# RWKV preparation of half 0 run beside the GLU blocks of the odd projection

## The reference

```
def odd_layer(x, ...):
    p = rms_norm(x, norm_g) @ w_in
    u, z_c, feat, z_d = split_cols(p, ODD_SIZES)
    y_c = jax.nn.gelu(s5_ssm(u, ...) + d_skip * u)
    g_a, g_b = jnp.split(y_c @ w_glu, 2, axis=-1)
    o_c = g_a * jax.nn.sigmoid(g_b) * jax.nn.silu(z_c)
    prev = jnp.pad(feat, ((0, 0), (1, 0), (0, 0)))[:, :-1]
    feat = feat + (prev - feat) * mu
    r, k, v, wd, ad = split_cols(feat, (512, 512, 512, 64, 64))
    o_d = rwkv7_time_mix(r, k, v, wd, ad, ...) * jax.nn.silu(z_d)
    return x + jnp.concatenate([o_c, o_d], axis=-1) @ w_out

def rwkv7_time_mix(r, k, v, wd, ad, ...):       # its start, what "preparation" computes
    w = -jax.nn.softplus(-(w0 + jnp.tanh(wd) @ w2)) - 0.5
    decay = jnp.exp(-jnp.exp(w))
    a = jax.nn.sigmoid(a0 + ad @ a2)
    kk = l2norm((k * k_k).reshape(bsz, T, H, Dh))
    k = k * (1.0 + (a - 1.0) * k_a)
    ...                                          # scan over tokens, group norm
    bonus = jnp.sum(rh * kh * r_k, axis=-1, keepdims=True) * vh
```

## Time and profile before

| | |
|---|---|
| median of three runs | 1521.49 us |
| the profiled execution | 1514.38 us, of which span 1512.6 us |
| PE busy | 1300.0 us (86%) |
| DVE busy | 891.8 us (59%) |
| ACT busy | 480.4 us (32%) |
| POOL busy | 308.6 us (20%) |
| projection of the odd layer, last matmul | about 1049.2 us |
| stage of preparation half 0 | 1053.2 to 1110.6 us |
| stage of `invert` half 0 and preparation half 1 | 1110.6 to 1206.8 us |

### The profile page before, as it was taken

How to read it: one execution, slowest core, us unless ns; L and a number is a source line. 1 busy time by engine, 2 the same in 40 slices (tenths; PEclk the granted TensorE clock), 3 DMA queues, 4 the chain that set the end, 5 groups by cost and what they waited for, 6 DMA issues and landing times. The chain is left out here.

```text
span 1512.6 us, 20654 instructions
## 1 busy us (share of the span) xinstructions
PE 1300.0 (86%) x8498; PEld 1079.1 (71%) x8498; DVE 891.8 (59%) x1191; ACT 480.4 (32%) x822; POOL 308.6 (20%) x156
## 2 busy tenths in 40 slices
PE   4999999899779869959997999998343798999698
PEld 4677888778569848848886888886122587889587
DVE  5277754920266573159975664943778787265841
ACT  5234254221346651132431122321652312122310
POOL 2232212211023372031211111220300400000420
PEclk9999999989899969989999999999655699689899
DMA  5212112320300032232331435221000000010523
GB/s 185 43 43 66 42 36 71 97 71 15 140 22 2 2 139 79 103 81 86 98 99 47 114 79 167 63 75 66 0 1 1 1 1 2 13 45 2 195 84 111
DMA packets 117558, 97.79 MB, mean 65 GB/s; under 512 B 37016, under 2 KB 102680, under 8 KB 117336
## 3 DMA queue, kind: packets, MB, share of 16 engines
q1 hardware_dynamic: 103832, 77.45, 17.1%
q10 hardware_dynamic: 13632, 19.01, 3.8%
HBM read 70.23 MB, written 24.51 MB: 63 GB/s over the span
## 5 line engine op out<-in xcount | busy, mean ns | idle before, releaser
L167 PE MATMUL banks<-xt_lo,w_hi 128*128 128x512 f32 x816 | 323.3, 396 | 6.3 <-POOL w_lo L497 6.3
L168 PE MATMUL banks<-xt_hi,w_lo 128*128 128x512 f32 x816 | 319.7, 392 | 0.0
L169 PE MATMUL banks<-xt_hi,w_hi 128*128 128x512 f32 x816 | 319.4, 391 | 0.0
L497 POOL TENSOR_TENSOR w_lo<-features,w_hi 128x1024 fp32r<-128x1024 f32 x55 | 149.4, 2717 | 525.6 <-ACT w_hi L506 525.6
L167 PEld LDWEIGHTS banks<-xt_lo,w_hi 128*128 128x128 f32 x816 | 154.4, 189 | 41.9 <-POOL w_lo L497 6.8
L169 PEld LDWEIGHTS banks<-xt_hi,w_hi 128*128 128x128 f32 x816 | 154.4, 189 | 32.9
L168 PEld LDWEIGHTS banks<-xt_hi,w_lo 128*128 128x128 f32 x816 | 154.6, 189 | 31.2
L550 ACT ACTIVATE temporaries<-banks 128x1024 f32<-128x1024 f32 x47 | 56.0, 1192 | 328.3 <-PE banks L169 320.3
L506 ACT ACTIVATE w_hi<-features 128x1024 fp32r<-128x1024 f32 x55 | 57.8, 1054 | 27.9 <-PE banks L169 26.7
L167 PE MATMUL banks<-xt_lo,oout_mh 128*128 128x512 f32 x128 | 50.8, 397 | 12.6 <-DVE xt_lo L1581 12.6
L295 PE MATMUL banks<-temporaries,features 128*128 128x128 f32 x256 | 35.7, 299 | 26.3 <-DVE temporaries L272 26.3
(11 more groups left out here) (451 smaller groups left out, 2618.8 us busy)
## 6 DMA issues: line engine op xcount, KB each, us to landing
features<-in_even_w_in SPq DMA_DIRECT2D x26, 512.0 KB, 3.8
features<-in_odd_w_in SPq DMA_DIRECT2D x25, 512.0 KB, 4.3
features<-in_x SPq DMA_DIRECT2D x8, 512.0 KB, 7.4
even_gates<-temporaries ACTq DMA_DIRECT2D x8, 512.0 KB, 2.6
features<-even_gates SPq DMA_DIRECT2D x8, 512.0 KB, 8.9
features<-in_even_w_out SPq DMA_DIRECT2D x8, 512.0 KB, 3.4
temporaries<-in_x SPq DMA_DIRECT2D x8, 512.0 KB, 4.7
h_between_layers<-features SPq DMA_DIRECT2D x8, 512.0 KB, 2.9
```

The costliest lines, as they stand in the source:

```text
L167: nc.tensor.matmul(out, w[0], x[1], start=start, stop=False)
L168: nc.tensor.matmul(out, w[1], x[0], start=False, stop=False)
L169: return nc.tensor.matmul(out, w[0], x[0], start=False, stop=stop)
L497: nc.gpsimd.tensor_tensor(wl[n % 2], wr[n % NW], wh[n % 2].bitcast(F32), ALU.subtract).then_inc(low, 1)
```

## The change

The v3 block is put ahead of the four GLU blocks (it is block 24 now, the GLU blocks are 25 to 28), so that all RWKV features and the normed input are done with when the GLU begins. A GLU block is now two units: all matmuls of the gate part into banks 2 and 3, then all of the value part into banks 0 and 1. Banks 4 to 7 are free, and the preparation of half 0 is put beside the GLU blocks in them, with the due times of `BESIDE_GLU`; its stage of its own is gone. Its tiles move into the area in which the normed input lay. For this the v3 block is written into a temporary, and the preparation of half 1 copies it to its place with one ACT instruction more. Of the semaphores, 33 are now cleared on POOL during the projection, and those of the projection and of preparation half 0 (90) at the start of the `invert` stage, where 32 were cleared before.

```diff
+                    def glu_unit(part):
+                        for h in range(2):
+                            for k in range(WB):
+                                hs, kw = slice(h * 512, (h + 1) * 512), WB * part + k
+                                last = three_passes(nc, co.ps[:, 2 * part + h, :], (wh[n % 2][:, kw, :], wl[n % 2][:, kw, :]),
+                                                    (glu["x"][0][k][:, hs], glu["x"][1][k][:, hs]), k == 0, k == WB - 1)
+                        return last
+
                     if glu_no[n] == 0:
                         pe.wait_ge(glu["low"], WB)
...
+                    else:
+                        pe.wait_ge(tanhed, post_no[n - 1] + 1)
+                    glu_unit(1).then_inc(gates_made, 1)
+                    aside.upto(n - 0.5)
+                    if glu_no[n] == 0:
+                        pe.wait_ge(evacuated, evac_no[n - 1] + 1)
+                    else:
+                        pe.wait_ge(finished, post_no[n - 1] + 1)
+                    last = glu_unit(0)
...
+                    if glu_no[n]:
+                        spill(n - 1)
+                    act.wait_ge(gates_made, glu_no[n] + 1)
+                    act.wait_ge(finished, post_no[n])
+                    nc.scalar.activation(t_.rearrange("p (h t) -> p h t", h=2), banks(2), ACT.Tanh, scale=0.25).then_inc(tanhed, 1)
+                    aside.upto(n - 0.25)
...
+BESIDE_GLU = dict(
+    tensor=dict(gates=(24.5, 25), sums=25.5, bonus=(25.5, 26), spread=26.5, pairs=lambda c: 29),
+    scalar=dict(start=24, gates=(24.75, 25.5), root=25.75, decay=(25.75, 26.5), high=26, slices=lambda c: 29),
+    gpsimd=dict(shift=(27, 27.5), rate=(28, 28), zero=29),
+    vector=dict(start=24, scan=(24.75, 25.5), centre=(25, 25.5), keys=(25, 25.5), root=25.75, low=26, decay=(26, 27), normal=(26.75, 26.75),
+                second=(27, 27.5), late=(27, 27.5), kept=lambda c: 29))
...
-    banks = lambda i: co.ps[:, 2 + 2 * (i % 3):4 + 2 * (i % 3), :]
+    banks = lambda i: co.ps[:, 2 + 2 * (i % 3):4 + 2 * (i % 3), :] if half else co.ps[:, 4 + 2 * (i % 2):6 + 2 * (i % 2), :]
...
+            if not half and i >= 2:
+                pe.wait_ge(tanhed, i - 1)
...
-            if c >= 3:
-                pe.wait_ge(kept, c - 2)
+            if c >= (3 if half else 2):
+                pe.wait_ge(kept, c - 2 if half else c - 1)
...
+        if half:
+            nc.scalar.activation(x.v[:, 1, :], x.v3_made, ACT.Copy).then_inc(v_placed, 1)
...
-    blocks += [(P * b, "glu", oc[b]) for b in range(WB)] + [(at("v", 3), "shift", v[3])]
+    blocks += [(P * b, "glu", oc[b]) for b in range(WB)]
...
+    cleared = clearing(co, at=2.5, done=(first_load, last_load))
...
+    project(co, "op", a["odd_w_in"][0], blocks, mu=a["rwkv_mu"][0], beside=together(s5, r7_prepare(co, first, BESIDE_GLU), cleared),
...
-    side_by_side(co, clearing(co), r7_prepare(co, first, 0))
-    side_by_side(co, clearing(co), invert(co, "ri0", first.n_st, R7_INVERT[0]), r7_prepare(co, second, 33))
+    side_by_side(co, clearing(co), invert(co, "ri0", first.n_st, R7_INVERT[0]), r7_prepare(co, second, beside_preparation(33)))
```

More of the change, by code:

```diff
@@ L97, in sem, with done_sems @@
         return handle
+    def done_sems(self, first, last):
+        old, self.taken = self.taken[:first] + self.taken[last:], self.taken[first:last]
+        return old
     def old_sems(self):
@@ L556, in _ @@
                     spill(n)
-                if n in post_no:
+                if n in post_no and n not in glu_no:
                     if kind == "conv":
@@ L2146, in clearing, with beside_preparation, r7_prepare @@
     return dict(gpsimd=gpsimd, old=old)
-def r7_prepare(co, x, d):
+def beside_preparation(d):
+    return dict(
+        tensor=dict(gates=(0, 0), sums=8, bonus=(d + 6.5, d + 12.5), spread=d + 14.5, pairs=lambda c: d + 30 + c),
+        scalar=dict(start=0, gates=(1, 8), root=9, decay=(d + 8, d + 14), high=d + 13, slices=lambda c: d + 31 + c),
+        gpsimd=dict(shift=(d + 6, d + 12), rate=(d + 17, d + 19), zero=d + 26),
+        vector=dict(start=0, scan=(d, d + 6), centre=(d + 2, d + 8), keys=(d + 4, d + 10), root=d + 12, low=d + 13.5, decay=(d + 15, d + 18.5), normal=(d + 16.5, d + 17.5),
+                    second=(d + 22, d + 25), late=(d + 23.5, d + 26.5), kept=lambda c: d + 30.5 + c))
+BESIDE_GLU = dict(
[4 more added lines that the diff above has]
+                second=(27, 27.5), late=(27, 27.5), kept=lambda c: 29))
+def r7_prepare(co, x, paces):
     nc = co.nc
@@ L2205, in tensor @@
         for j in range(2):
-            if j:
-                pe.wait_ge(bout, 1)
+            if not half or j:
+                pe.wait_ge(bout, j if half else j + 1)
             for h in range(2):
                 hs = slice(512 * h, 512 * h + 512)
-                nc.tensor.matmul(banks(1 + j)[:, h, :], pairs[:, j, :], low[:, hs], start=True, stop=False)
-                last = nc.tensor.matmul(banks(1 + j)[:, h, :], pairs[:, j, :], high[:, hs], start=False, stop=True)
+                nc.tensor.matmul(banks(spread_at[j])[:, h, :], pairs[:, j, :], low[:, hs], start=True, stop=False)
+                last = nc.tensor.matmul(banks(spread_at[j])[:, h, :], pairs[:, j, :], high[:, hs], start=False, stop=True)
             last.then_inc(spread, 1)
         for c in range(NT):
-            yield d + 30 + c
+            yield at["pairs"](c)
             if c == 0:
```

199 lines of the change are left out of this document (114 added, 85 removed).

## The result

The changed kernel takes 1479.88 us (median of four, 1474.99 to 1484.29) against 1522.13 on the same chip: a ratio of 0.973, 95% interval 0.971 to 0.9745. The prediction was 1494.2 us and a gain of 27.3; the gain is 42.2 here, and in two more measurements of the same kernel 35.5 (ratio 0.979, 0.974 to 0.984) and 35.2 (0.976, 0.974 to 0.978). The profiled execution took 1474.99 us, with a span of 1473.2.

A forecast was written before the change was run, and what follows sets the result against it. TensorE bounds the GLU blocks; the preparation's own stage is a chain of waits. Added 14.4 + tail 15.4 - 61.4 replaced = -31.6; clears +4.3 make -27.3, so 1521.49 becomes 1494.2 us, range 1489 to 1505.

The forecast's parts named there:

- the rival of the clock: GLU stretch: waits before the units bring TensorE to 1.2 GHz; all at half would cost 55 us; chance 0.05.
- The sum inside the GLU blocks: TensorE from v3's last matmul to the last GLU matmul: 43.5 + 14.4 added = 57.9 us.
- logits: Preparation's 8 matmuls of 512 columns among the GLU units: 5.2 us on TensorE, between 3.4 (low) and 6.8.
- sums: Preparation's sums of squares on TensorE among the GLU units: 1.1 us added.
- bonus: Preparation's 4 bonus matmuls on TensorE among the GLU units: 3.5 us added.
- spreading: Preparation's 8 spreading matmuls on TensorE among the GLU units: 1.7 us added at full clock.
- Waits: TensorE among the GLU units, before logits, squares and spreading: 0.9, 1.2 and 0.8, together 2.9 us.
- The tail: From TensorE's last GLU matmul to the next stage: 2.6 + 8.9 + 3.9 = 15.4 us.
- The store: Last GLU block's store, behind ScalarE's slices in the tail: 3.9 us from issue to next stage.
- The clears: Start of the inversion's stage: 58 more semaphore clears on GpSimd delay VectorE's first line and cost 4.3 us.
- The rival in which they hide: Inversion's stage: the later start from the clears is absorbed, total 1489.9 us; chance 0.10.
- VectorE did not become the bound: Rival in the GLU stretch: GpSimd blocks VectorE for 16.8 us instead of 8, making it the bound, 1503.0 us; chance 0.15.

The follow-up runs named there:

- the pause of 3225 columns: Kernel before plus a stage of one GpSimd memset of 3225 columns ahead of the stage of state half 0: 1524.59 us, ratio 1.005 (0.999 to 1.011).

## Why the prediction was wrong

The step that failed is the last sentence of its paragraph on clearing: "The half 1 program and everything behind it are otherwise the same." The instructions are; their time is not. By the mean of the three profiles of the changed kernel, the state stage and what follows take 292.5 us against 302.0: 9.5 us of gain that the sum did not have. Without them the time would have been near 1491, inside the range. I had weighed the clock only inside the GLU blocks, where it could cost, and not in stages further on, where TensorE runs groups of 32x32 products between waits and the granted clock was 0.94 and 0.86. The 0.94 that the prediction held against the rival of the clock comes from a row that ends at 1288.0, just ahead of the 18 us at 0.59 shown above; the whole stage had 0.86. From the profile of before alone the sign could not have been worked out, but a bound could: the stage of state half 0 had about 31 us at half clock (112.5 x 0.14 x 2), and a few of them belonged in the range.

Point by point:

- **Up to the next stage.** In six profiles with the instructions of before, the memset L756 starts at 1119.9 us in the mean (1113.1 to 1126.1); in seven with those of the changed kernel the same memset, L784, starts at 1089.4 (1085.2 to 1093.1). The difference, 30.5, stands against 27.3 of the forecast. The stages ahead move by several us from one execution to the next in either kernel, so that the whole span of one pair cannot tell these apart. Read by its stages the first pair agrees: 34.1 us less on the way to the next stage (104.8 to 70.7) and 4.0 more in that stage make 30.1, while all ahead of the last five blocks took 2.4 us longer (997.3 against 994.9).
- **The sum inside the GLU blocks was right.** 57.9 us forecast, 58.8 in the row. TensorE added 11.1 against 11.5: logits 4.0 (5.2 forecast, the one term that had only a range, and near its low end of 3.4), sums 1.3 (1.1), bonus 3.9 (3.5), spreading 2.0 (1.7). Waits 3.5 against 2.9. Some 0.7 us of the row is in neither.
- **The tail was too long by 3.4.** The kept chunks begin 2.0 us behind TensorE's last unit (2.6 forecast), and chunks and slices take 8.9, as forecast. The store was mis-sized. The 3.9 us of the earlier trace rows count from its issue at 1049.33 to the next stage at 1053.20, and I took them for the store's. But in the kernel before VectorE was still at work on v3, and ended 0.3 us ahead of the next stage:

```profile
1051.62 1.28 DVE L598 SCALAR_TENSOR_TENSOR features<-features,constants,temporaries 128x1024 f32<-128x1024 f32 x1
```

  The stores of this kind land 2.6 us after their issue (median of four in the profile of before), so that this one had landed at about 1051.9, an estimate. And I put the 3.9 us behind the slices. Here the last GLU result is there since 1068.94, the queue issues the store 1.9 us before the slices end, and from issue to the next stage it is 3.07 us (1075.81 to 1078.88); 1.2 of them lie in the open.
- **The clears were right.** 4.3 us forecast; the wait of L802 grew by 3.8, and the stage from 96.2 in the cut of the earlier trace rows (100.0 to the next stage's first memset) to 104.0. The rival in which they hide did not come.
- **VectorE did not become the bound.** It was busy 52.3 of 58.8 us. Some of its passes stood still beside GpSimd's, as in the earlier trace rows:

```profile
1024.68 3.22 POOL L521 TENSOR_TENSOR w_lo<-features,w_hi 128x1024 fp32r<-128x1024 f32 x1 [11.91 <-ACT w_hi L531]
1034.61 2.91 POOL L2343 TENSOR_TENSOR big<-big 128x1024 f32<-128x1024 f32 x1 [6.71 <-PE banks L2262]
```

```profile
1025.54 3.44 DVE L2388 TENSOR_TENSOR features<-features,big 128x1024 f32<-128x1024 f32 x1
1029.02 1.23 DVE L2389 TENSOR_TENSOR big<-features 128x1024 f32<-128x1024 f32 x1
1034.03 1.22 DVE L2388 TENSOR_TENSOR features<-features,big 128x1024 f32<-128x1024 f32 x1
1035.29 3.32 DVE L2389 TENSOR_TENSOR big<-features 128x1024 f32<-128x1024 f32 x1
```

  L2388 and L2389 take 1.2 us free, and 3.4 and 3.3 when a GpSimd pass began ahead of them. That agrees with the Trainium skill, "SBUF — State Buffer" (SBUF: two separate sides), on the lock of the pair of ports; it fell on a few passes, not on seven: with line 625 (3.30 us beside the first remainder) and one of line 2398 (1.84) VectorE stood some 7 us, where the forecast had 8.
- **The clock did not fall among the GLU units**, at 1.00 for 58.8 us with three short waits: for that stretch the rival was rightly small. What the Trainium skill tells in "TensorE: Matmul & The Clock Gate" (Part 1), a kernel that idles briefly and often and swings between the two levels, is what the state stages do, before the change as after: in the stage of state half 0 of the kernel before the clock falls five times behind the first rise and is at half for 30.6 us. I had it beside the wrong stage.

- **The range.** Its low end was to be the hidden clears with the low logits; that is 1489.9 less 1.8, 1488.1 and not 1489. The measured time lies below either.

In sum: 3.2 us too little for the part that the change touches, and 9.5 for the part that it doesn't. With the 27.3 forecast they make 40.0, among the measured gains of 35.2, 35.5 and 42.2.

Open: why the kernel before, and the changed one with its stage of its own, find the rise at 0.9 us in all of three profiles, while the changed kernel varies. Whether the placement by itself makes the good alignments more frequent, or the three profiles were lucky, these runs don't tell.

## What to carry to other kernels

A stage with much time at the half clock is not a constant of the program. When work ahead of it moves, its length can jump either way; here the sum of this stage and what follows went from 290.2 to 312.0 us for the same instructions in them, with 302.0 before: put that stage's time at half clock into the range, and look at it first when a result doesn't fit the sum. Price a change by the stages that it touches, over several profiles, and judge small edits (here, clears and a store of 1 to 6 us in the trace) by the trace of their stage when the whole time spreads by more. And when a gap behind a DMA's issue is priced as the DMA's, look at what every engine does in it: here another engine's pass filled the gap, and a store listed behind passes was issued before they ended.

## What the runs showed of the hardware

- The rise of the granted clock came at the same place of the stage to 0.03 us in three executions of two programs, in which the stage began at 1210.6, 1217.5 and 1222.5 us. What brings it there was not found, and the changed kernel had it at 1.06, 2.28 and 13.6 us.
- An added stage with one GpSimd memset of 1.66 us did not make the kernel before slower: 1511.45 against 1518.34 us (0.9965, 0.993 to 0.9999), with 10.6 us less in the two stretches behind it.
- The same VectorE and ScalarE work, in place to 0.1 us for 77 us, was followed by a return of the clock at 83.0 us in one program and at 86.3 in the other.
- One program can have two times: the pause of 3225 columns gave 1514 and 1534 us, four runs each, with mean clocks of 0.915 to 0.920 and 0.904 to 0.908.
